# Handing more of the fp32 split to GpSimd, and spacing the router's steps, in a two-block transformer kernel

## The chip, the cores and the metric

The kernel runs on one core of one Trainium2 chip. The metric is the device time of one execution in microseconds (us), as a median over runs; smaller is better.

## The reference, cut to what matters

Two blocks work on 256 tokens of width 1024. The change touches only the PEER feed-forward that closes each of the two layers of the second block (128 x 128 experts, 8 heads, 16 experts per head):

```
def peer_ffn(x, w_query, sub_keys, down, up):      # T = 256, H = 8, K = 16
    q = (xt @ w_query).reshape(T, H, 2, 64)
    s = einsum('thcd,cnd->thcn', q, sub_keys)      # scores of 2 x 128 keys
    sv, si = top_k(s, K)
    cand_s = (sv[:, :, 0, :, None] + sv[:, :, 1, None, :]).reshape(T, H, K * K)
    cand_i = (si[:, :, 0, :, None] * 128 + si[:, :, 1, None, :]).reshape(T, H, K * K)
    top_s, pos = top_k(cand_s, K)
    idx, gate = take_along_axis(cand_i, pos), softmax(top_s)
    a = einsum('thkd,td->thk', down[idx], x)       # down, up: 16384 x 1024
    c = gate * gelu(a)
    return einsum('thk,thkd->td', c, up[idx])
```

## The kernel before, in words

**Weights as slots.** All weights are streamed from HBM in the order of their use and cut into 765 slots of 128 x 1024 fp32. Every slot is split into a high part `whi` (ScalarE copies the raw slot to fp32r, `hi`, L312) and a low part `wlo` (raw minus high, `lo`, L331). TensorE then multiplies three products per tile (`three`, L349 to L351). There are three buffers of `whi` and `wlo`, so the split of slot i waits until TensorE has used slot i-3. The low part is made by VectorE, except for the slots named in the set `ON_POOL`, which GpSimd (POOL) makes; both engines walk through the slots in order. GpSimd has nothing else to do in the PEER stages until they end.

**The PEER stage** of a layer has 264 slots, from 201 in layer 0 and from 501 in layer 1: 8 of `w_query`, then 128 of `down`, then 128 of `up`. The experts are not gathered: all 16384 activations are computed. In the down phase a loop over pairs p = 0 to 63 takes slots i = 209 + 2p and i + 1 (layer 0), and ScalarE puts the gelu of the result into `AST` (L2606). In the up phase the loop runs over 62 pairs and a tail; ScalarE (`CH`, L2589) and VectorE (`CL`, L2808) split the scaled activations for each pair. `ON_POOL` holds, in layer 0, slots 212 to 239 and every second slot from 339 to 401.

**Routing** runs beside the down phase. `route_at(p)` names the steps that VectorE takes in pair p, after its `lo(i+3)` and `lo(i+4)`:

- `keys(q, 1..5)`, q = 0 to 3: top 16 of the key scores, with MAX8, FIND_INDEX8, MATCH_REPLACE8. TensorE supplies the scores by `scores(q)` (L2484).
- `pick(tt, 0..5)` for each half tt of the tokens: `CD` (sums of candidates, L2690 to L2696), their top 16, and in segment 5 `TB` (L2704), the scores less the largest.
- ScalarE takes the exponential of that (`pick(tt, 5)`, L2576).
- `pick(tt, 6)` waits for it and then normalizes; segments 7 to 9 and 11 to 13 turn positions into expert numbers with `count` (L2670, L2674): 60 small instructions per tt, each with two inputs in SBUF.
- TensorE turns the three tables over (`tables(tt)`, L2494), after pairs 22 and 29. It works in order: what comes behind in its queue waits for VectorE's last `count` and the copy L2759. ScalarE copies the turned tables out after pairs 23 and 30, and VectorE splits the gates in segment 20 at pairs 24 and 31.

**Gates.** From pair 32 on, in down and up, `gates(s)` for 64 groups of 8 tokens: TensorE L2504, then on VectorE L2799 (`AST` times gates) and `build(s+2)` (`OI` L2782, `EQ` L2786, `OJ` L2791). `gates_at` names the pairs; in three of them (n = 47, 74, 84) there are two groups.

Of the kernel before, what the change touches and what calls it, by code (L numbers as in the profile page):

```python
# [67 lines left out]
ON_POOL = set(range(1, 14, 2)) | set(range(71, 100, 2))  # L68
for _s in (165, 465):
    ON_POOL |= set(range(_s + 2, _s + 31, 2))  # L70
for _s in (201, 501):
    ON_POOL |= set(range(_s + 11, _s + 39)) | set(range(_s + 138, _s + 202, 2))


class Book:
# [81 lines left out]
class Program:  # L157
# [2274 lines left out]
        t.spill = self.nc.dram_tensor(f"x_spill{l}", (P, 2 * D), F32, kind="Internal").ap()  # L2432
        return t

    def route_at(self, p):

        if p < 10:
            return [("keys", s // 5, s % 5 + 1) for s in (2 * p, 2 * p + 1)]  # L2440
        if p < 14:
            tt = (p - 10) // 2
            return [("pick", tt, 3 * (p % 2) + s) for s in range(3)]
        if p < 28:
            tt = (p - 14) // 7
            return [("pick", tt, (6, 7, 8, 9, 11, 12, 13)[(p - 14) % 7])]
        return []

    def gates_at(self, n):

# [23 lines left out]
    def peer_pe(self, e, t):  # L2474
        k, PS, n, tag = self.k, self.ps, t.n, t.tag
        self.norm_turned(n)

        def scores(q):
            tt, half = q // 2, q % 2
            for h in range(4 * half, 4 * half + 4):  # L2480
                b = 4 + h // 2
                for w in k.late((tag, "qh", h), (tag, "sk in"), *(self.free[b] if h % 2 == 0 else [])):
                    e.wait_ge(*w)
                m = e.matmul(PS[:, b, (h % 2) * 256:(h % 2) * 256 + 256], t.QH[:, h, tt * 128:tt * 128 + 128], t.SK[:, :],  # L2484
                             start=True, stop=True)
                self.free[b] = [(tag, "keys", q, 5, 7)]
            m.then_inc(*k.inc("pe_keys", (tag, "scores", q)))

        def tables(tt):
            self.bank(e, 2 + tt)  # L2490
            for j, what in enumerate(("oi", "oj", "g")):
                for w in k.late((tag, what, tt)):
                    e.wait_ge(*w)
                m = e.transpose(PS[:, 2 + tt, 128 * j:128 * j + 128], t.TB[:, tt, j, :], self.ident[:, :])  # L2494
            m.then_inc(*k.inc("pe_keys", (tag, "tables turned", tt)))
            self.free[2 + tt] = [(tag, "table", tt, 2)]

        def gates(s):
            b = 2 + s % 2
            for w in k.late((tag, "one i", s), (tag, "one j", s, 0), (tag, "one j", s, 1), *self.free[b]):  # L2500
                e.wait_ge(*w)
            for x in range(8):
                for p in range(2):
                    m = e.matmul(PS[:, b, 64 * x:64 * x + 64], t.OI[s % 2][:, x // 2, :, x % 2], t.OJ[s % 2][:, p, x // 2, :, x % 2],  # L2504
                                 start=p == 0, stop=p == 1)
            m.then_inc(*k.inc("pe_gates", (tag, "gates", s)))
            self.free[b] = [(tag, "scaled", s)]

        def query(h):
            b = h % 2 if h > 1 else 4 + h  # L2510
            if h == 0:
                self.chan_pair(e, t.slot, n, [PS[:, x, 0:T] for x in (4, 5)], [4, 5])
            elif h > 1:
                self.bank(e, b)
                self.chan(e, t.slot + h, n, PS[:, b, 0:T])
            self.free[b] = [(tag, "qh", h)]

        for h in range(8):
            query(h)
        scores(0)  # L2520
        for p in range(64):
            b, i = p % 2, t.down + 2 * p
            self.bank(e, b)
            self.chan(e, i, n, PS[:, b, 0:T])
            self.chan(e, i + 1, n, PS[:, b, T:2 * T], ahead=p == 63)
            self.free[b] = [(tag, "gelu", p)]
            if p in (1, 4, 6):
                scores((1, 4, 6).index(p) + 1)
            if p in (22, 29):
                tables(p // 29)  # L2530
            for s in self.gates_at(p):
                gates(s)
        rows = (tag, t.up, t.CH, t.CL, range(128), lambda c: [(tag, "ch", c // 2), (tag, "cl", c // 2)], (4, 5, 6, 7))
        for p in range(62):
            for s in self.gates_at(64 + p):
                gates(s)
            for x in range(2):
                self.rows_main(e, *rows, 2 * p + x)
        self.rows_main(e, *rows, 124)
        self.rows_first(e, *rows)  # L2540
        self.rows_second(e, *rows)
        for h in range(2):
            self.rows_third(e, *rows, h)
        self.free[4:8] = [[("x", n + 1, tt, h)] for tt in range(2) for h in range(2)]
        if t.l == 0:
            for tt in range(2):
                self.norm_turn(e, n + 1, tt)
# [7 lines left out]
    def peer_act(self, e, t):  # L2555
        k, PS, n, tag = self.k, self.ps, t.n, t.tag
# [12 lines left out]
                self.hi(e, t.slot + 4)  # L2569

        def pick(tt, seg):
            if seg == 5:
                g = t.TB[:, tt, 2, :].rearrange("p (h k) -> p h k", k=16)
                for w in k.late((tag, "less", tt)):
                    e.wait_ge(*w)
                e.activation(g, g, ACT.Exp, bias=0.0, scale=1.0).then_inc(*k.inc("act_keys", (tag, "exp", tt)))  # L2576
            if seg == 19:
                q = slice(128 * tt, 128 * tt + 128)
                for j, (o, scale) in enumerate(((t.IT, 1.0), (t.JT, 1.0), (t.GF, SCALE))):
                    for w in k.late((tag, "tables turned", tt), (tag, "spilled"), ("hl", n, 7)):  # L2580
                        e.wait_ge(*w)
                    e.activation(o[:, q], PS[:, 2 + tt, 128 * j:128 * j + 128], ACT.Copy, bias=0.0,
                                 scale=scale).then_inc(*k.inc("act_keys", (tag, "table", tt, j)))
# [10 lines left out]
        for p in range(64):  # L2594
            b, i = p % 2, t.down + 2 * p
            self.hi(e, i + 3)
            if p == 63:
                part(0)
                part(1)
            self.hi(e, i + 4)  # L2600
            late = [(tag, "keys", 3, 5, 7)] if 2 * p == t.on_keys else []
            if 2 * p == t.on_tables:
                late = [(tag, "tables", 0), (tag, "tables", 1)]
            for w in k.late(("used", i + 1), *late):
                e.wait_ge(*w)
            e.activation(t.AST[:, p, :, :].rearrange("p t a -> p a t"), PS[:, b, :].rearrange("p (a t) -> p a t", a=2),  # L2606
                         ACT.Gelu_apprx_tanh, bias=0.0, scale=1.0).then_inc(*k.inc("act_down", (tag, "gelu", p)))
            if p in (11, 13):
                pick(p // 13, 5)
            if p in (23, 30):  # L2610
                pick(p // 30, 19)
        for p in range(62):
            part(p + 2)
            for x in range(2):
# [7 lines left out]
    def peer_dve(self, e, t):  # L2622
        k, PS, n, tag = self.k, self.ps, t.n, t.tag
# [52 lines left out]
        def pick(tt, seg):  # L2676
            s = t.SV[:, tt, :, :].rearrange("p (h c) k -> p h c k", c=2)
# [20 lines left out]
            if 1 <= seg < 6:  # L2698
                best((tag, "top", tt), seg - 1, lambda r: cd[:, r, :], lambda r: t.TV[:, tt, r, :], lambda r: t.PI[:, tt, r, :],
                     lambda r: cd[:, r, :], range(8), [(tag, "sums", tt)])  # L2700
            if seg == 5:
                for w in k.late((tag, "top", tt, 4, 7)):
                    e.wait_ge(*w)
                e.tensor_tensor(g, t.TV[:, tt, :, :], t.TV[:, tt, :, 0:1].to_broadcast([P, 8, 16]),  # L2704
                                ALU.subtract).then_inc(*k.inc("dve_pick", (tag, "less", tt)))
            if seg == 6:
                for w in k.late((tag, "exp", tt)):
                    e.wait_ge(*w)
                e.tensor_reduce(t.sm[:, tt, 0:8], g, AX, ALU.add).then_inc(*k.inc("dve_pick", (tag, "total", tt)))
# [43 lines left out]
                k.same((*col, "sum", -2), (*col, "sum", -1))  # L2753
            if 11 <= seg < 14:
                count(tt, col, range(1, 16), 1, 5 * (seg - 11))
            if seg == 13:
                for w in k.late((*col, "sum", 14)):
                    e.wait_ge(*w)
                e.tensor_copy(oj, acc).then_inc(*k.inc("dve_pick", (tag, "oj", tt)))  # L2759
            if seg == 20:  # L2760
                q = slice(128 * tt, 128 * tt + 128)
# [51 lines left out]
        for p in range(64):  # L2813
            i = t.down + 2 * p
            self.lo(e, i + 3)
            if p == 63:
                part(0)
                part(1)
            self.lo(e, i + 4)
            for kind, q, seg in self.route_at(p):  # L2820
                (keys if kind == "keys" else pick)(q, seg)
            if p in (24, 31):
                pick(p // 31, 20)
            if p == 31:
                build(0)
                build(1)
            for s in self.gates_at(p):
                gates(s)
# [288 lines left out]
```

## Time and profile before

| what | before |
|---|---|
| median of 3 runs | 2531.83 us (2531.47 to 2534.66) |
| profiled execution: its time / span | 2534.66 us / 2532.8 us |
| TensorE busy | 2441.3 us (96%) |
| VectorE busy | 1816.0 us (72%) |
| ScalarE busy | 1192.0 us (47%) |
| GpSimd busy | 536.9 us (21%) |
| the PEER stages | about 765 to 1560 us and 1740 to 2533 us |

TensorE's time is close to the whole; the other engines' shares are averages over stages in which they have quite different loads.

### The profile page before, as it was taken

To read this page: it belongs to the slowest core of one execution; us is meant where nothing else is said; L and a number is where in the kernel's file an instruction comes from. 1 tells how busy PE (TensorE), PEld (TensorE's weight loads), DVE (VectorE), ACT (ScalarE), POOL (GpSimd) and SP (SyncE) were. 2 spreads that over 40 slices of the span, in tenths; PEclk is the share of its full clock that TensorE was granted. 3 is DMA by queue.
4 is the path that set the end of the run, shared out by engine and by line. 5 is a ranking of instruction groups with operands and counts; after the bars stand their busy time and mean duration, and the time that the engine had idled before them with its cause. 6 is when DMAs were issued, how large, how long until landed. Compare 5 with 4: busy or idle time off the path is not lost.

```text
span 2532.8 us, 43179 instructions
## 1 busy us (share of the span) xinstructions
PE 2441.3 (96%) x17718; PEld 2224.5 (88%) x17718; DVE 1816.0 (72%) x3408; ACT 1192.0 (47%) x1665; POOL 536.9 (21%) x374
## 2 busy tenths in 40 slices
PE   7999798998999999999999999999999999999999
PEld 7987778987879999999778887888999999877887
DVE  8787946656545687777998555745777777999555
ACT  3545545445445544444444555454454444444444
POOL 3023321003423700001333001340720000333000
PEclk9999999999999999999999999999999999999999
DMA  9696534654324455444445555324455444444554
GB/s 386 205 374 220 183 114 160 216 201 156 117 100 169 170 180 184 167 167 167 167 164 195 196 197 181 113 101 152 168 184 182 169 166 167 172 169 174 202 197 150
DMA packets 73045, 456.03 MB, mean 180 GB/s; under 512 B 9099, under 2 KB 15371, under 8 KB 20754
## 3 DMA queue, kind: packets, MB, share of 16 engines
q1 hardware_dynamic: 72162, 452.21, 49.8%
q8 instruction: 142, 2.33, 0.4%
q0 software_dynamic: 688, 1.06, 0.3%
q14 instruction: 53, 0.43, 0.0%
HBM read 449.17 MB, written 4.06 MB: 179 GB/s over the span
## 4 chain that ended last, share of the span: by engine, by line
PE 75%; DVE 18%; ACT 3%; issue 2%; POOL 1%; DMA 0%; SPq 0%; DVEq 0%; POOLq 0%; ACTq 0%
PE ps L349 23%; PE ps L351 23%; PE ps L350 23%; DVE OI L2782 4%; DVE wlo L331 3%; PE ps L2504 2%; DVE AST L2799 1%; DVE raw L342 1%; DVE CL L2808 1%; ACT whi L312 1%; PE ps L377 1%; DVE OJ L2791 1%; DVE XB L1182 1%; DVE EQ L2786 1%; ACT xn L454 1%
## 5 line engine op out<-in xcount | busy, mean ns | idle before, releaser
L312 ACT ACTIVATE whi<-raw 128x1024 fp32r<-128x1024 f32 x765 | 809.6, 1060 | 1143.8 <-PE ps L351 1094.4
L331 DVE TENSOR_TENSOR wlo<-raw,whi 128x1024 fp32r<-128x1024 f32 x593 | 736.6, 1245 | 522.7 <-ACT whi L312 522.3
L349 PE MATMUL ps<-HH,whi 128*128 128x256 f32 x3016 | 867.5, 288 | 8.2 <-DVE wlo L331 4.4
L350 PE MATMUL ps<-HL,whi 128*128 128x256 f32 x3016 | 856.6, 284 | 0.0
L351 PE MATMUL ps<-HH,wlo 128*128 128x256 f32 x3016 | 856.4, 284 | 0.0
L331 POOL TENSOR_TENSOR wlo<-raw,whi 128x1024 fp32r<-128x1024 f32 x172 | 421.5, 2451 | 1167.4 <-ACT whi L312 1167.4
L349 PEld LDWEIGHTS ps<-HH,whi 128*128 128x128 f32 x3016 | 580.4, 192 | 13.8 <-issue 8.4
L350 PEld LDWEIGHTS ps<-HL,whi 128*128 128x128 f32 x3016 | 580.7, 193 | 0.8
L351 PEld LDWEIGHTS ps<-HH,wlo 128*128 128x128 f32 x3016 | 580.3, 192 | 0.5
L349 PE MATMUL ps<-whi,CH 128*128 128x512 f32 x1024 | 405.3, 396 | 7.3 <-DVE wlo L331 7.3
L350 PE MATMUL ps<-wlo,CH 128*128 128x512 f32 x1024 | 400.0, 391 | 0.0
L351 PE MATMUL ps<-whi,CL 128*128 128x512 f32 x1024 | 400.0, 391 | 0.0
L349 PEld LDWEIGHTS ps<-whi,CH 128*128 128x128 f32 x1024 | 193.1, 189 | 47.0 <-ACT whi L312 8.9
L351 PEld LDWEIGHTS ps<-whi,CL 128*128 128x128 f32 x1024 | 193.0, 188 | 40.6
L350 PEld LDWEIGHTS ps<-wlo,CH 128*128 128x128 f32 x1024 | 193.2, 189 | 38.2
L2782 DVE TENSOR_TENSOR OI<-iota,IT 128x1024 f16<-128x1024 bf16 x128 | 182.7, 1427 | 0.0
L2808 DVE SCALAR_TENSOR_TENSOR CL<-AST,CH 128x512 fp32r<-128x512 f32 x128 | 101.5, 794 | 9.2 <-ACT CH L2589 8.9
L462 POOL TENSOR_SCALAR st<-st 128x1 f32<-128x1 f32 x20 | 9.8, 492 | 460.8 <-ACT xn L454 258.8
L2791 DVE TENSOR_TENSOR OJ<-EQ,GP 128x512 f16<-128x512 f16 x256 | 97.4, 421 | 4.4
L342 DVE CUSTOM_DVE_ANT_0 raw<-raw,cb 128x1024 f32<-128x1024 f32 x72 | 92.2, 1318 | 0.0
L2799 DVE TENSOR_TENSOR AST<-AST,ps 128x512 f32<-128x512 f32 x128 | 87.0, 680 | 6.2 <-PE ps L2504 4.2
L349 PE MATMUL ps<-whi,HH 128*128 128x256 f32 x288 | 85.1, 296 | 0.0
(390 smaller groups left out, 2735.5 us busy)
## 6 DMA issues: line engine op xcount, KB each, us to landing
raw<-in_down SPq DMA_DIRECT2D x128, 1024.0 KB, 4.8
raw<-in_up SPq DMA_DIRECT2D x128, 1024.0 KB, 4.8
raw<-in_w_in SPq DMA_DIRECT2D x41, 1024.0 KB, 4.8
raw<-in_ffn_gu SPq DMA_DIRECT2D x36, 1024.0 KB, 5.0
raw<-in_w_ada SPq DMA_DIRECT2D x28, 1024.0 KB, 6.7
raw<-in_ffn_d SPq DMA_DIRECT2D x22, 1024.0 KB, 5.6
raw<-in_w_out SPq DMA_DIRECT2D x12, 1024.0 KB, 4.8
raw<-in_w_ada SPq DMA_DIRECT2D x16, 512.0 KB, 13.3
```

What stands on the lines that cost most here:

```text
L312: e.activation(self.whi[:, i % NSPLIT, :], self.raw_of(i), ACT.Copy, bias=0.0, scale=1.0).then_inc(*k.inc("w_hi", ("hi", i)))
L331: e.tensor_tensor(self.wlo[:, n, :], self.raw_of(i), self.whi[:, n, :].bitcast(F32), ALU.subtract).then_inc(*k.inc("w_lo_pool" if pool els ...
L342: e.tensor_tensor_reduce(out=raw[:, a, :], in0=raw[:, a, :], in1=self.cb[:, :], scale=1.0, scalar=0.0, op0=ALU.mult, op1=ALU.add, accum_ou ...
L349: e.matmul(out, lh, rh, start=first, stop=False)
L350: e.matmul(out, lh, rl, start=False, stop=False)
L351: return e.matmul(out, ll, rh, start=False, stop=stop)
L377: t = e.matmul(outs[j], part[:, s], h[:, c, :], start=first and not (j and one), stop=stop and (j == 1 or not one))
L2504: m = e.matmul(PS[:, b, 64 * x:64 * x + 64], t.OI[s % 2][:, x // 2, :, x % 2], t.OJ[s % 2][:, p, x // 2, :, x % 2], start=p == 0, stop=p == 1)
L2782: e.tensor_tensor(t.OI[c][:, :, :, :], self.iota[:, :, :].unsqueeze(1).to_broadcast([P, 4, 128, 2]), spread(t.IT, 128), ALU.is_equal).then ...
L2791: e.tensor_tensor(t.OJ[c][:, p, :, :, :], t.EQ[:, :, :, :], spread(t.GP[:, p, :], 64), ALU.mult).then_inc(*k.inc("dve_gates", (tag, "one j ...
L2799: e.tensor_tensor(c, c, PS[:, b, :].rearrange("p (t j a) -> p j t a", a=2, j=32), ALU.mult).then_inc(*k.inc("dve_gates", (tag, "scaled", s)))
L2808: e.scalar_tensor_tensor(lo, t.AST[:, p, :, :].rearrange("p t a -> p a t"), 1.0 / SCALE, hi.bitcast(F32), ALU.mult, ALU.subtract).then_inc ...
```

## The change

`ON_POOL` grows in the PEER stages: in layer 0 from 212..239 and every second slot of 339..401 to all slots 213..275 and every second one of 277..453 (first slot of each pair). Slot 212 goes to VectorE. Layer 1 is the same, 300 slots later.

The routing steps get another order in time: `route_at(n)` gives the steps 2n+1 and 2n+2 of one list, of 24 steps of `keys` (6 for each q) and 42 of `pick` (21 for each tt). So `scores(1..3)` come after pairs 2, 5, 8 (before: 1, 4, 6), the exponentials after pairs 14 and 25 (before: 11, 13), `tables(0)` and `tables(1)` after pairs 20 and 30 (before: 22, 29), ScalarE's copies after 21 and 31 and segment 20 at pairs 21 and 32 (before: 24, 31). Segment 6 now holds both `TB` and the normalization, L2759 stands in segment 14. The instructions themselves stay the same. On VectorE, all of `pick(1, ..)` now comes behind segment 20 of tt 0; before, segments 0 to 5 of tt 1 came ahead of segment 6 of tt 0, and `TB` ahead of each wait for the exponential by a pair or more.

```
 for _s in (201, 501):
-    ON_POOL |= set(range(_s + 11, _s + 39)) | set(range(_s + 138, _s + 202, 2))
+    ON_POOL |= set(range(_s + 12, _s + 75)) | set(range(_s + 76, _s + 253, 2))
...
-    def route_at(self, p):
-        if p < 10:
-            return [("keys", s // 5, s % 5 + 1) for s in (2 * p, 2 * p + 1)]
-        if p < 14:
-            tt = (p - 10) // 2
-            return [("pick", tt, 3 * (p % 2) + s) for s in range(3)]
-        if p < 28:
-            tt = (p - 14) // 7
-            return [("pick", tt, (6, 7, 8, 9, 11, 12, 13)[(p - 14) % 7])]
-        return []
+    def route_at(self, n):
+        out = []
+        for s in (1 + 2 * n, 2 + 2 * n):
+            if s < 24:
+                out.append(("keys", s // 6, s % 6))
+            elif s < 66:
+                out.append(("pick", (s - 24) // 21, (s - 24) % 21))
+        return out
...
-            if p in (1, 4, 6):
-                scores((1, 4, 6).index(p) + 1)
-            if p in (22, 29):
-                tables(p // 29)
+            for kind, q, seg in self.route_at(p):
+                if kind == "keys" and seg == 0:
+                    scores(q)
+                if kind == "pick" and seg == 17:
+                    tables(q)
...
-            if p in (11, 13):
-                pick(p // 13, 5)
-            if p in (23, 30):
-                pick(p // 30, 19)
+            for kind, q, seg in self.route_at(p):
+                if kind == "pick":
+                    pick(q, seg)
...
-            if seg == 5:
+            if seg == 6:
...
-            if seg == 6:
...
-            if seg == 13:
+            if seg == 14:
...
-            if p in (24, 31):
-                pick(p // 31, 20)
```

## Rows read from the trace of the kernel before

**Rows 1.** Windows: engines' busy time, TensorE's granted clock, DMA share, GB/s.
```profile
818.00:860.00 42.00, 42.00 (x339) 41.59 (x339) 31.10 (x204) 18.24 (x21) 31.94 (x15) 1.00 0.49 171
1085.00:1184.00 99.00, 99.00 (x997) 98.36 (x996) 75.63 (x117) 41.13 (x47) 0.00 (x0) 1.00 0.47 169
1184.00:1250.00 66.00, 66.00 (x459) 54.04 (x458) 64.63 (x76) 30.57 (x36) 26.40 (x11) 1.00 0.48 171
1250.00:1320.00 70.00, 68.17 (x455) 54.79 (x453) 68.36 (x85) 29.13 (x33) 26.63 (x11) 0.98 0.44 156
```

**Rows 2.** Waits of the whole run: total us, times, longest us.
```profile
PE ps L349 <- DVE wlo L331: 11.7, 9, 2.6
```

**Rows 3.** Timeline of ScalarE (start, duration) in the down phase: gelu and exponential.
```profile
870.14 0.31 ACT L2576 ACTIVATE TB<-TB 128x128 f32<-128x128 f32 x1
...
914.29 0.62 ACT L2606 ACTIVATE AST<-ps 128x512 f32<-128x512 f32 x1
920.05 0.62 ACT L2606 ACTIVATE AST<-ps 128x512 f32<-128x512 f32 x1
```

**Rows 4.** Costliest groups of the page: count, busy us, mean ns.
```profile
L312 ACT ACTIVATE whi<-raw 128x1024 fp32r<-128x1024 f32 x765 | 809.6, 1060 | 1143.8 <-PE ps L351 1094.4
```

**Rows 5.** Timeline of GpSimd in the down phase, with idle time before each.
```profile
848.16 2.52 POOL L331 TENSOR_TENSOR wlo<-raw,whi 128x1024 fp32r<-128x1024 f32 x1 [0.41 <-ACT whi L312]
851.11 2.40 POOL L331 TENSOR_TENSOR wlo<-raw,whi 128x1024 fp32r<-128x1024 f32 x1 [0.42 <-ACT whi L312]
...
856.86 2.40 POOL L331 TENSOR_TENSOR wlo<-raw,whi 128x1024 fp32r<-128x1024 f32 x1 [0.55 <-ACT whi L312]
```

**Rows 6.** Timeline of VectorE over the same stretch.
```profile
847.87 2.96 DVE L2690 TENSOR_TENSOR CD<-SV 128x128 f32<-128x128 f32 x5
...
851.11 1.00 DVE L2632 MAX8 TV<-CD 128x8 f32<-128x50 f32 x8
...
857.36 2.06 DVE L2704 TENSOR_TENSOR TB<-TV 128x128 f32<-128x128 f32 x1
```

**Rows 7.** Timeline of VectorE: one pair of count, the last copy.
```profile
892.78 0.29 DVE L2670 SCALAR_TENSOR_TENSOR T<-PF,DL 128x128 f32<-128x128 f32 x1
893.11 0.29 DVE L2674 TENSOR_TENSOR AC<-AC,T 128x128 f32<-128x128 f32 x1
893.32 0.28 DVE L2670 SCALAR_TENSOR_TENSOR T<-PF,DL 128x128 f32<-128x128 f32 x1
...
924.08 0.23 DVE L2759 COPY TB<-AC 128x128 f32<-128x128 f32 x1
```

**Rows 8.** Groups of VectorE's instructions, 870 to 980 us: busy us, mean ns.
```profile
L331 DVE TENSOR_TENSOR wlo<-raw,whi 128x1024 fp32r<-128x1024 f32 x34 | 41.2, 1222 | 28.1 <-ACT whi L312 28.0
L2674 DVE TENSOR_TENSOR AC<-AC,T 128x128 f32<-128x128 f32 x60 | 17.5, 292 | 2.1
L2670 DVE SCALAR_TENSOR_TENSOR T<-PF,DL 128x128 f32<-128x128 f32 x60 | 17.1, 284 | 0.1
```

**Rows 9.** Timeline of TensorE: the tables of the first tt.
```profile
930.35 0.49 PE L2494 MATMUL ps<-ident,TB 128*128 128x128 f32 x3
```

**Rows 10.** Windows after idle time of TensorE, at its lower clock.
```profile
301.00:313.00 12.00, 3.14 (x24) 2.94 (x24) 11.80 (x15) 2.58 (x4) 5.51 (x2) 0.82 0.64 231
313.00:319.00 6.00, 5.47 (x22) 4.49 (x23) 4.78 (x13) 4.92 (x10) 0.00 (x0) 0.50 0.15 63
1257.00:1261.00 4.00, 3.52 (x9) 2.79 (x10) 3.96 (x8) 0.00 (x0) 0.00 (x0) 0.58 0.63 221
```

**Rows 11.** Groups: building the one-hot tables without GpSimd (down) and beside it (up).
```profile
L2782 DVE TENSOR_TENSOR OI<-iota,IT 128x1024 f16<-128x1024 bf16 x17 | 11.6, 685 | 0.0
L2782 DVE TENSOR_TENSOR OI<-iota,IT 128x1024 f16<-128x1024 bf16 x11 | 28.4, 2580 | 0.0
```

**Rows 12.** Timeline of VectorE where two groups of gates fall in one pair.
```profile
1253.92 3.41 DVE L331 TENSOR_TENSOR wlo<-raw,whi 128x1024 fp32r<-128x1024 f32 x1
```

**Rows 13.** Timeline of GpSimd at the same place.
```profile
1253.54 2.71 POOL L331 TENSOR_TENSOR wlo<-raw,whi 128x1024 fp32r<-128x1024 f32 x1 [4.14 <-ACT whi L312]
```

More of the change, by code:

```diff
@@ L2700, in pick @@
                      lambda r: cd[:, r, :], range(8), [(tag, "sums", tt)])
-            if seg == 5:
+            if seg == 6:
                 for w in k.late((tag, "top", tt, 4, 7)):
```

## The prediction, made before the change was run

> **What bounds the kernel now.** I read the windows over the stretches of one PEER stage first [rows 1]. TensorE is busy for all of the 42, 99 and 66 us of the first three, so in the down phase (with routing, then with gates) and at the start of the up phase it is the bound. Next the waits [rows 2]: TensorE's waits for a low part come to 11.7 us in the whole run. So the work that the change lifts from VectorE is work for which hardly anything waits. The gain to be had is small, and what counts is whether somebody new becomes late. A pair takes 5.76 us in the down phase (920.05 less 914.29) [rows 3], a slot 2.88 us.
>
> **What GpSimd's split does to VectorE.** GpSimd takes 2.40 us for one slot [rows 5], where VectorE takes 1.22 us [rows 8]. If it makes every slot, it is busy for 2.40 of 2.88 us and leaves gaps of 0.41 to 0.55 us [rows 5]. TensorE stayed busy in that regime [rows 1], so GpSimd's own pace is no loss. Now lay the two timelines side by side [rows 5, 6]. `TB`, 128 elements, starts on VectorE at 857.36 and takes 2.06 us, to 859.42; GpSimd's split ran from 856.86 to 859.26. A `count` instruction of 128 elements takes 0.28 to 0.29 us [rows 8]. So `TB` stood still until GpSimd had ended and finished 0.16 us later. The five `CD` sums took 2.96 us, to 850.83, 0.15 us behind the end of the split at 850.68. The one-hot `OI` shows the same: 0.685 us without GpSimd, 2.58 us beside it [rows 11]. These instructions read two operands from SBUF. MAX8, with one input, ran its eight in 1.00 us right beside a split [rows 6].
>
> The Trainium skill ("SBUF — State Buffer", Who interferes with whom) states this as a rule: a VectorE instruction with two SBUF inputs and a GpSimd instruction that reads SBUF exclude each other, the first keeps the shared ports for its whole length, and the other one blocks. The trace agrees (2.06 against 0.29 us).
>
> **Part 1, slots 213 to 275 on GpSimd.** Slots 240 to 275 are the new ones; they are needed during pairs 15 to 33. Just there VectorE runs the `count` chains, 60 instructions with two SBUF inputs for each tt. Before, no split of GpSimd's ran beside them. Saved on VectorE: 36 x 1.22 = 44 us per layer, worth nothing on TensorE's path, since it did not wait there. What it costs, for each tt:
>
> - The work between the exponential and the tables: 30 pairs of `count` at 0.54 us (892.78 to 893.32) [rows 7] are 16.2 us, and 15 other small instructions at about 0.26 us are 3.9 us: 20.1 us in 75 instructions, some 0.27 us each, if nobody is in the way.
> - How much of it goes through while GpSimd works: in each cycle of 2.88 us the gap is 0.48 us. The blocked instruction goes first, a second follows, at times a third; then GpSimd has the ports again. It isn't kept out by a queue of small instructions: in the middle of the five `CD` GpSimd's split came out at 2.52 us, 0.12 us over the usual 2.40 [rows 5]. So 2 to 3 instructions per cycle. From the `CD` sums alone one could read 4, but all but the first of these have 24 to 64 elements (8 heads by 3 to 8); I take 2.25 of 128 elements, 0.6 us of work, and keep 2 (0.53 us) and 4 (1.06 us) as bounds.
> - tt 0: the exponential is made after pair 14 instead of 11, so it ends at 870.45 + 3 x 5.76 = 887.7 us [rows 3]. TensorE comes to `tables(0)` two pairs earlier than at 930.35 [rows 9], at 918.8 us. When it stops there, one more slot is copied (1.06 us [rows 4]) and split (2.40 us) before GpSimd falls idle for want of a free buffer: 3.5 us. By then 31.1 + 3.5 = 34.6 us have passed, 12 cycles, with 12 x 0.6 = 7.2 us of work. 12.9 us are left, and VectorE does them at its full speed, since GpSimd stands still. **Wait of TensorE: 3.5 + 12.9 = 16.4 us.**
> - tt 1: now all of `pick(1, ..)` waits behind segment 20 of tt 0, but the exponential after pair 25 still comes later than its input: from the resumption at about 935 us, pair 21 and ScalarE's table take to about 945, segment 20, the sums and four rounds of MAX8 and its kin some 15 us more, and pair 25 ends near 966. The exponential ends 3.4 us behind its pair (870.45 against 930.35 - 11 x 5.76 = 867.0) [rows 3, 9], `tables(1)` stand five pairs on: 28.8 - 3.4 = 25.4 us, and 3.5, are 10 cycles with 6.0 us of work. 14.1 us are left. **Wait: 17.6 us.**
> - After each wait TensorE starts at half its clock. After 12 us in which it was busy for 3.14 only, the window from 313 to 319 us shows 0.50, the 1.2 GHz level, for nearly 6 us; from 1257 to 1261 us, after one of the short stalls of part 3, it is 0.58, or 3.4 of 4 us at the lower level [rows 10]. I estimate 3.4 to 5.4 us at half speed after each wait, a loss of half of that, 1.7 to 2.7 us; I take 2.4.
>
> Per layer 16.4 + 17.6 + 4.8 = 38.8 us. Layer 1 has the same instructions at the same relative times. Two layers: **77.6 us**.
>
> **Part 2, the spacing of the steps.** `scores(1..3)` one to two pairs later and the exponential three pairs later cost nothing by themselves: VectorE was through with tt 0 at 924.3 us [rows 7], 6 us ahead of the tables. But these 6 us, the cover, are used up: without any blocking, tt 0 would be ready at 887.7 + 20.1 = 907.8, 11 us ahead of the tables at 918.8. With blocking it would need over 90 us. The spacing, which shortens the time to the tables, thus adds to part 1; it costs nothing without it. Slot 212 on VectorE delays `keys(0)` by a few us; the banks of `scores(2)` are asked for only after pair 5. Nothing.
>
> **Part 3, every second slot from 277 to 335, beside the gates.** VectorE has one split less (1.22 us) and up to one blocked `OI` more (2.58 against 0.69, 1.9 us) per pair; a pair with gates lasts 6.3 us. Behind the waiting `OI` stand `EQ`, `OJ` and the next low part. In the up phase just this arrangement, with `CL` on top, left TensorE busy for 66 of 66 us [rows 1], with less time per pair. So nothing; if the pair with two groups (n = 47) stalls as the ones in the up phase do, where a low part on VectorE took 3.41 us behind GpSimd's split [rows 12, 13], that is 1.83 us idle (70 less 68.17 [rows 1]) and 1.7 us for the clock, 3.5 us per layer, 7 in all.
>
> **Part 4, every second slot from 403 to 453.** VectorE is lightly loaded there; a blocked `CL` costs it under 2 us in a pair and saves one split. Nothing.
>
> **Sum.** The profiled execution took 2534.7 us, its span 2532.8; it is the slowest of the three runs, 2.8 us above the median. Its span plus 77.6 is 2610, against the median 2531.8 + 77.6 = 2609 us. With 4 instructions per cycle the waits are 10.8 and 12.9 us, and with 1.7 for the clock the sum is 2 x 27.1 = 54, so 2586. With 2 per cycle 17.2 and 18.3, with 2.7 for the clock and 7 us of part 3 it is 2 x 40.9 + 7 = 89, so 2621.
>
> **The rivals.**
>
> - *The small instructions aren't held.* Only larger or strided ones would wait. Then tt 0 is ready at 907.8 us, ahead of the tables, and nothing changes: 2532 us. For it: the first of the five `CD` passed. Against it: `TB`, 128 elements just like `count`. One page of the Trainium skill ("Advanced Engine Details and Errata", Mode Summary) has a note that names only VectorE's two-port modes as interfering with GpSimd, which would leave the fp32 additions of `count` alone; this trace speaks against reading it so.
> - *GpSimd is the one kept out.* If the chain of `count` holds the ports from end to end, GpSimd loses 20.1 us per tt, TensorE has two slots in hand (5.8 us) and waits 14.3 us for low parts: 4 x (14.3 + 2.4) = 67, 2599 us. Against it: the split of 2.52 us. It differs in what TensorE is seen waiting for.
> - *Faster.* The four stalls of a doubled group of gates, 1.8 us and about 1.7 us for the clock each, 14 us in all, might go, if another phase between VectorE and GpSimd let the low part through: 2518 us. It decides only if the tables don't wait at all. The slots there are assigned as before, so nothing asks for it.
>
> **How the numbers follow.** The forecast, waits at the tables that add 54 to 89 us: 0.78. GpSimd kept out, 2599: 0.08. Not held, 2532: 0.09. Faster, 2518: 0.03. Another cause of a smaller loss: 0.02. What a measurement of this kernel can tell from no change is about 0.2%, 5 us. Faster 0.03, same 0.09, slower 0.88. The range is the forecast's with some room above for what follows late tables (the first `build`s): 2580 to 2632. It leaves out the unchanged and the faster case, and a little on either side.
>
> **What would show it.** TensorE idle for 12 to 18 us ahead of L2494, twice in each layer; `count` instructions of about 2.5 us between 888 and 920 us, some two per split of GpSimd's, then a run of undisturbed ones while TensorE and GpSimd stand still. The down phase with gates without idle time of TensorE. The prediction is wrong if TensorE is found waiting for low parts, if `count` keeps its 0.28 us beside GpSimd, or if 5 or more get through in each gap.

## The result, and the profile after

| | before | after |
|---|---|---|
| median | 2533.24 us (4 runs) | 2606.99 us (4 runs) |
| profiled execution: time / span | 2534.66 / 2532.8 us | 2605.91 / 2603.7 us |
| ratio, 95% interval | | 1.0292 (1.028 to 1.0305) |

Slower by 74 us, against a forecast of 77 (2609 us). In the profiled executions the span grew by 70.9 us. One execution of e9 below ran in a slower state (2672.52 us at a granted clock of 0.843, the others at 0.984 to 0.987); it counts in the median of e9 but not in its ratio. Line numbers differ by a few between the kernels: `tables` is L2494 before and L2491 here, `count` L2670 and L2674 before, L2667 and L2671 here.

The page of the changed kernel, engine by engine:

```profile
PE 2451.5 (94%) x17718; PEld 2232.7 (86%) x17718; DVE 1926.8 (74%) x3224; ACT 1191.3 (46%) x1665; POOL 1012.4 (39%) x558
```

GpSimd has 476 us more, and VectorE, from which 184 splits were taken, is busy for 111 us more instead of less. The timelines below show why: an instruction that stands still counts as busy. TensorE's waits for the tables, which were not in the list of before (total us, times, longest):

```profile
PEld ps L2491 <- DVE TB L2755: 36.2, 4, 9.1
PE ps L2491 <- DVE TB L2755: 35.0, 4, 8.8
PEld ps L2491 <- DVE TB L2738: 25.8, 4, 7.2
PE ps L2491 <- DVE TB L2738: 25.0, 4, 7.0
```

The timeline of TensorE, layer 0, answers to [rows 9]; the number in brackets is the idle time ahead. `tables` first waits for the row numbers (`TB` of L2738), then for the column numbers (L2755):

```profile
924.30 0.48 PE L2491 MATMUL ps<-ident,TB 128*128 128x128 f32 x1 [5.51 <-DVE TB L2738]
933.53 0.69 PE L2491 MATMUL ps<-ident,TB 128*128 128x128 f32 x2 [8.75 <-DVE TB L2755]
999.82 0.47 PE L2491 MATMUL ps<-ident,TB 128*128 128x128 f32 x1 [7.00 <-DVE TB L2738]
1009.05 0.69 PE L2491 MATMUL ps<-ident,TB 128*128 128x128 f32 x2 [8.76 <-DVE TB L2755]
```

So 14.3 us for tt 0 and 15.8 us for tt 1, 30.0 us in this layer. The waits of the whole run are 60.0 us, so layer 1 has 30.0 us too. Of the 70.9 us of the span 10.9 are left, 5.4 per layer. Nearly all of that is the clock: for the same 17718 matmuls TensorE is busy for 10.2 us more than before (2451.5 against 2441.3), 5.1 per layer, where the forecast had 4.8. The windows around and behind the two waits, and the stretch of gates in the down phase (busy time of PE, PEld, DVE, ACT and POOL, then the granted clock, as in [rows 1]):

```profile
918.00:935.00 17.00, 2.73 (x15) 2.24 (x14) 14.58 (x44) 1.57 (x2) 4.02 (x2) 0.64 0.18 62
934.00:940.00 6.00, 6.00 (x44) 6.00 (x43) 0.00 (x0) 1.06 (x1) 0.73 (x1) 0.80 0.01 3
1012.00:1018.00 6.00, 6.00 (x41) 6.00 (x41) 0.46 (x2) 1.16 (x2) 1.96 (x1) 0.76 0.01 3
1085.00:1185.00 100.00, 100.00 (x1028) 99.31 (x1027) 91.64 (x101) 41.40 (x48) 44.35 (x16) 1.00 0.47 164
```

And what VectorE and GpSimd do ahead of the wait (VectorE's timeline, then its groups and GpSimd's between 887.5 and 918.5 us), to lay beside [rows 7, 8]:

```profile
908.47 0.28 DVE L2667 SCALAR_TENSOR_TENSOR T<-PF,DL 128x128 f32<-128x128 f32 x1
908.79 2.38 DVE L2671 TENSOR_TENSOR AC<-AC,T 128x128 f32<-128x128 f32 x1
911.09 0.28 DVE L2667 SCALAR_TENSOR_TENSOR T<-PF,DL 128x128 f32<-128x128 f32 x1
911.40 2.46 DVE L2671 TENSOR_TENSOR AC<-AC,T 128x128 f32<-128x128 f32 x1
913.79 0.28 DVE L2667 SCALAR_TENSOR_TENSOR T<-PF,DL 128x128 f32<-128x128 f32 x1
```

```profile
L2671 DVE TENSOR_TENSOR AC<-AC,T 128x128 f32<-128x128 f32 x12 | 14.0, 1168 | 0.4
L2667 DVE SCALAR_TENSOR_TENSOR T<-PF,DL 128x128 f32<-128x128 f32 x12 | 12.2, 1020 | 0.0
```

```profile
L331 POOL TENSOR_TENSOR wlo<-raw,whi 128x1024 fp32r<-128x1024 f32 x12 | 29.3, 2443 | 5.3 <-ACT whi L312 5.3
```

Two or three instructions go through for each split, and one of them carries the length of the split. In 31 us VectorE gets 24 of its 60 `count` instructions done, where an undisturbed chain needs 16 us for all 60. GpSimd's last split before the stop runs from 920.01 to 922.45 us. Behind it the chain runs free, while TensorE and GpSimd stand still, to the copy that TensorE waits for:

```profile
922.64 0.29 DVE L2671 TENSOR_TENSOR AC<-AC,T 128x128 f32<-128x128 f32 x1
...
932.92 0.29 DVE L2671 TENSOR_TENSOR AC<-AC,T 128x128 f32<-128x128 f32 x1
933.25 0.23 DVE L2755 COPY TB<-AC 128x128 f32<-128x128 f32 x1
```

### The profile page after: what moved, and what is told of

It is laid out like the page before. It is cut to its first block, busy times and chain, and to the rows that moved or that the text cites. A ratio compares the mean times of both kernels' runs of the same rounds, so it can differ in the third digit from the quotient of the medians.

```text
span 2603.7 us, 43291 instructions
## 1 busy us (share of the span) xinstructions
PE 2451.5 (94%) x17718; PEld 2232.7 (86%) x17718; DVE 1926.8 (74%) x3224; ACT 1191.3 (46%) x1665; POOL 1012.4 (39%) x558
## 4 chain that ended last, share of the span: by engine, by line
PE 68%; DVE 24%; ACT 3%; issue 2%; POOL 1%; DMA 1%; SPq 0%; DVEq 0%; POOLq 0%; ACTq 0%
PE ps L349 21%; PE ps L351 20%; PE ps L350 20%; DVE OI L2778 4%; DVE wlo L331 3%; DVE AC L2671 3%; DVE T L2667 3%; PE ps L2501 2%; ACT whi L312 1%; DVE AST L2795 1%; DVE raw L342 1%; DVE CL L2804 1%; DVE OJ L2787 1%; PE ps L377 1%; DVE EQ L2782 1%
## 5 line engine op out<-in xcount | busy, mean ns | idle before, releaser
L331 POOL TENSOR_TENSOR wlo<-raw,whi 128x1024 fp32r<-128x1024 f32 x356 | 894.3, 2512 | 1047.8 <-ACT whi L312 1047.7
L331 DVE TENSOR_TENSOR wlo<-raw,whi 128x1024 fp32r<-128x1024 f32 x409 | 511.9, 1253 | 270.3 <-ACT whi L312 269.8
L2804 DVE SCALAR_TENSOR_TENSOR CL<-AST,CH 128x512 fp32r<-128x512 f32 x128 | 191.5, 1497 | 102.9 <-ACT CH L2587 102.6
L2782 DVE TENSOR_TENSOR EQ<-iota,JT 128x512 f16<-128x512 bf16 x128 | 197.0, 1539 | 0.0
```

The source lines that it names most:

```text
L331: e.tensor_tensor(self.wlo[:, n, :], self.raw_of(i), self.whi[:, n, :].bitcast(F32), ALU.subtract).then_inc(*k.inc("w_lo_pool" if pool els ...
L2782: e.tensor_tensor(t.EQ[:, :, :, :], self.iota[:, js, :].unsqueeze(1).to_broadcast([P, 4, 64, 2]), spread(t.JT, 64), ALU.is_equal).then_inc ...
L2804: e.scalar_tensor_tensor(lo, t.AST[:, p, :, :].rearrange("p t a -> p a t"), 1.0 / SCALE, hi.bitcast(F32), ALU.mult, ALU.subtract).then_inc ...
```

## The experiments

Ten kernels, beside the kernel before on the same chip. `before` stands for that kernel, `after` for the changed one; medians in us, ratios to before.

| kernel | median | ratio (95%) |
|---|---|---|
| e1: GpSimd's slots alone | 2577.35 | 1.018 (1.0163 to 1.0197) |
| e2: spacing alone | 2558.45 | 1.0101 (1.0083 to 1.0118) |
| e3: after, 240..275 back on VectorE | 2559.63 | 1.0106 (1.0089 to 1.0123) |
| e4: after, every second of 240..275 | 2575.16 | 1.0165 (1.0148 to 1.0182) |
| e5: after, operands in PSUM | 2549.77 | 1.0063 (1.0048 to 1.0078) |
| e8: e1, operands in PSUM | 2536.76 | 1.0007 (0.9998 to 1.0016) |
| e6: before, two slots more per layer | 2538.67 | 1.0017 (1.0008 to 1.0026) |
| e7: before, slots swapped | 2522.30 | 0.9956 (0.9942 to 0.9969) |
| e9: e8 with the swap of e7 | 2524.49 | 0.9954 (0.994 to 0.9969) |
| e10: before, slots beside gates and at the end | 2534.88 | 1.0002 (0.9994 to 1.0011) |

### e1: GpSimd's new slots alone

```diff
-    ON_POOL |= set(range(_s + 11, _s + 39)) | set(range(_s + 138, _s + 202, 2))
+    ON_POOL |= set(range(_s + 12, _s + 75)) | set(range(_s + 76, _s + 253, 2))
```

> The new set of GpSimd's slots alone, with the steps of the router spaced as before. If small instructions with two SBUF inputs stand still during a split (the theory), the tables are still late: VectorE starts tt 0 at 886.8 us, TensorE asks for them at 930.4, and 47 us at 0.6 us of work per 2.88 us leave 10 us to do, a wait of 14 us; much the same for tt 1; with the clock 33 us per layer, about 2598 us. If it was the spacing of the steps that cost the time (first rival), this kernel takes about 2532 us.

Measured 2577 us: not 2532, so the slots alone make the tables late, but 21 us less than worked out. The timeline shows the two waits of layer 0:

```profile
937.90 0.69 PE L2494 MATMUL ps<-ident,TB 128*128 128x128 f32 x2 [7.65 <-DVE TB L2759]
988.75 0.69 PE L2494 MATMUL ps<-ident,TB 128*128 128x128 f32 x2 [8.25 <-DVE TB L2759]
```

The expectation let VectorE begin the tables' work at 886.8 us, as before. It begins at 870.5, right behind ScalarE's exponential:

```profile
870.50 0.27 DVE L2709 TENSOR_REDUCE sm<-TB 128x8 f32<-128x128 f32 x1
...
871.25 2.43 DVE L2717 CAST PF<-PI 128x128 f32<-128x128 uint32 x1
...
873.91 2.54 DVE L2721 TENSOR_TENSOR DL<-SF 128x240 f32<-128x240 f32 x1
...
876.94 2.37 DVE L2670 SCALAR_TENSOR_TENSOR T<-PF,DL 128x128 f32<-128x128 f32 x1
```

With no low part of its own between the steps, nothing ties VectorE to the pair that TensorE is in, and the written order gives no times any more.

### e2: the new spacing of the router's steps alone

```diff
-    ON_POOL |= set(range(_s + 12, _s + 75)) | set(range(_s + 76, _s + 253, 2))
+    ON_POOL |= set(range(_s + 11, _s + 39)) | set(range(_s + 138, _s + 202, 2))
```

(in after)

> The new spacing of the steps alone, with GpSimd's slots as before. The theory: 2532 us, within 5, since VectorE has its 20 us of work for tt 0 done by about 913 us, before TensorE asks at 918.8. The first rival (the spacing costs the time: tables asked for sooner, tt 1 wholly behind tt 0): about 2607 us, with idle time of TensorE ahead of the tables.

Neither: 2558 us. TensorE does not wait for tables but, between 880 and 1000 us, for low parts:

```profile
PE ps L349 <- DVE wlo L331: 7.0, 5, 2.4
PEld ps L349 <- ACT whi L312: 4.9, 3, 1.7
PEld ps L349 <- issue: 4.4, 3, 2.6
PE ps L349 <- ACT whi L312: 1.2, 1, 1.2
```

VectorE's timeline there shows why:

```profile
900.84 2.35 DVE L331 TENSOR_TENSOR wlo<-raw,whi 128x1024 fp32r<-128x1024 f32 x2
903.11 0.28 DVE L2667 SCALAR_TENSOR_TENSOR T<-PF,DL 128x128 f32<-128x128 f32 x1
...
905.53 0.29 DVE L2671 TENSOR_TENSOR AC<-AC,T 128x128 f32<-128x128 f32 x1
905.74 2.35 DVE L331 TENSOR_TENSOR wlo<-raw,whi 128x1024 fp32r<-128x1024 f32 x2
```

The new spacing puts two segments of `count` (5.3 us) beside two splits (2.3 us) into a pair of 5.76 us; the old one put one segment there. The waits of the matmuls themselves sum to 8.2 us in this stage (7.0 and 1.2; those of `PEld` are the same gaps seen from the weight load); the span grew by 22.7 us, 11.3 per layer, and not all of it comes from the spacing. Counted from the first gelu of a layer (`AST`, L2606 before, L2604 here), the growth is 2.2 us ahead of the gelu of layer 0 (803.27 against 801.10 us), where the kernels do not differ, 7.9 from there to that of layer 1 (980.80 against 972.94), and 12.7 from there to the end (771.43 against 758.76). Layer 0 is thus accounted for by its waits; layer 1 has the same 8.2 us, and TensorE is busy for 4.4 us more, with a granted clock of 0.72 between 1896 and 1902 and between 2252 and 2258 us, where layer 1 of the kernel before shows no such drop.

### e3: the changed kernel without slots 240 to 275

```diff
-    ON_POOL |= set(range(_s + 12, _s + 75)) | set(range(_s + 76, _s + 253, 2))
+    ON_POOL |= set(range(_s + 12, _s + 39)) | set(range(_s + 76, _s + 253, 2))
```

> The changed kernel, but slots 240 to 275 of a layer back on VectorE; the slots beside the gates and at the end of the up phase stay on GpSimd. The theory: the whole loss goes, 2532 us within 5. Second rival (the blocked one-hot builds or CL beside the new slots from 277 on cost part of it): above 2540 us; every stall of a low part in the down phase would show as idle time of TensorE between 990 and 1184 us.

2560 us, 20 us above the bound named for the second rival, but for another reason: the waits are those of e2 (7.0 us for low parts between 880 and 1000 us), and between 990 and 1184 us TensorE has no idle time. Against e2 it is 1.2 us. As a test of the slots beside the gates it was badly built, since the new spacing costs 25 us by itself once VectorE makes the low parts; e10 repeats it cleanly.

### e4: every second one of slots 240 to 275

```diff
-    ON_POOL |= set(range(_s + 12, _s + 75)) | set(range(_s + 76, _s + 253, 2))
+    ON_POOL |= set(range(_s + 12, _s + 39)) | set(range(_s + 40, _s + 253, 2))
```

> The changed kernel, with only every second one of slots 240 to 275 on GpSimd. The theory: per pair of 5.76 us GpSimd holds the ports for 2.4 us and VectorE's own split takes 1.2, so 2.1 us are left for the router's work of 20.1 us; at the tables 9 to 11 us of it are left, waits of about 10 us each, and with the clock about 2580 us (2568 to 2590). If only an almost full GpSimd does harm (third rival: the gaps close when it is busy for 2.4 of 2.88 us), about 2532 us.

2575 us, within the range, but the path is not the expected one. There is no wait at the tables; between 880 and 1000 us TensorE waits for VectorE's low parts:

```profile
PEld ps L349 <- issue: 15.6, 5, 3.4
PE ps L349 <- DVE wlo L331: 14.8, 5, 3.2
```

The held `count` chains now stand in front of low parts in VectorE's own queue:

```profile
894.13 2.50 DVE L2667 SCALAR_TENSOR_TENSOR T<-PF,DL 128x128 f32<-128x128 f32 x1
...
899.84 2.46 DVE L2671 TENSOR_TENSOR AC<-AC,T 128x128 f32<-128x128 f32 x1
...
903.26 1.22 DVE L331 TENSOR_TENSOR wlo<-raw,whi 128x1024 fp32r<-128x1024 f32 x1
```

The time is no support for my working. It does answer the third rival: GpSimd is busy for only 2.4 of 5.76 us here, its split still holds a `count` instruction for 2.5 us, and the kernel is 17 us slower than e2, which has the same spacing.

### e5 and e8: one input of each count instruction in PSUM

```diff
-        t.DL = a("DL", [P, 2, 8, 2, 16])
+        t.DL = [self.ps[:, 4 + tt, 0:256].rearrange("p (h c k) -> p h c k", c=2, k=16) for tt in range(2)]
+        t.T1 = [[self.ps[:, 6 + tt, 128 * j:128 * j + 128] for j in range(2)] for tt in range(2)]
-        t.AC, t.T1 = a("AC", [P, 2, 128]), a("T1", [P, 2, 2, 128])
+        t.AC = a("AC", [P, 2, 128])
```

(The lines of the buffers alone. `DL` is an input of the first instruction of each `count` pair; `T1` is its output and an input of the second.)

> The changed kernel with DL and T1, one operand of each of the 120 count instructions of a layer, held in PSUM: the same instructions, GpSimd's slots and spacing. The theory (two operands in SBUF make an instruction stand still during a split): count takes about 0.3 us each again; of the 75 instructions of a tt some 15 still have two operands in SBUF or are held copies, 5 to 6 cycles of 2.9 us, so the tables are ready at 915 to 925 us and TensorE waits 0 to 7 us each: 2532 to 2560, about 2545 us. Rival (a split slows any VectorE instruction of a chain, wherever its operands lie): 2605 us again.

> The same move to PSUM in the kernel with the new set of GpSimd's slots and the old spacing (2577 us so far, tables late by 7.7 and 8.3 us). The theory: VectorE is ready with the tables of tt 0 by about 905 us, 25 us early: 2532 us within 5. Rival as before: 2577 us.

e5: 2550 us, 57 us better than after, 5 above the point expected and within the range. VectorE's groups between 887.5 and 918.5 us, and GpSimd's:

```profile
L2668 DVE SCALAR_TENSOR_TENSOR ps<-PF,ps 128x128 f32<-128x128 f32 x30 | 8.7, 291 | 0.1
L2672 DVE TENSOR_TENSOR AC<-AC,ps 128x128 f32<-128x128 f32 x30 | 8.6, 288 | 1.0
L2742 DVE SCALAR_TENSOR_TENSOR TB<-TB,AC 128x128 f32<-128x128 f32 x1 | 2.5, 2450 | 0.0
L2748 DVE TENSOR_SCALAR AC<-SF 128x128 f32<-128x128 f32 x1 | 2.4, 2386 | 0.0
```

```profile
L331 POOL TENSOR_TENSOR wlo<-raw,whi 128x1024 fp32r<-128x1024 f32 x12 | 28.9, 2405 | 5.7 <-ACT whi L312 5.7
```

Beside the same 12 splits all 60 `count` instructions run, at 0.29 us, and GpSimd's splits are back at 2.405 us from 2.443. What stands still in this stretch has its inputs in SBUF: two of them (L2742) or, in two `TENSOR_SCALAR`s, only one (L2748). The 16 us that e5 is still above the kernel before have a place: the tables of tt 0 are ready in time (916.8 us), those of tt 1 are late by 3.6 us in each layer, and the clock follows.

```profile
PE ps L2492 <- DVE TB L2756: 7.2, 2, 3.6
```

e8 has the move with the old spacing: TensorE never waits for tables, and of e1's 44 us 3.3 are left; the interval holds 1. In the profiled execution of e8 even these arise before the PEER stages: its first gelu comes at 804.56 instead of 801.10 us, and from there to the end both kernels take 1731.6 to 1731.7 us. This settles the mechanism: same instructions, same order, same splits, another place of one input. (In the first instruction of a pair the output moved as well; in the second, L2672, only the input did, and it is at 0.288 us just the same.)

### e10: the slots beside the gates and at the end, alone

```diff
-    ON_POOL |= set(range(_s + 11, _s + 39)) | set(range(_s + 138, _s + 202, 2))
+    ON_POOL |= set(range(_s + 11, _s + 39)) | set(range(_s + 76, _s + 253, 2))
```

> The kernel before with only the slots beside the gates (every second one of 277 to 335) and at the end of the up phase (403 to 453) added to GpSimd's. The forecast priced these two parts at nothing: 2533 us within 5. Second rival (the blocked one-hot builds make a low part or a group of gates late): more than 2540 us.

No difference (1.0002), as priced. One of the builds is held in each pair, `EQ` and not `OI` as forecast (groups of VectorE, 1085 to 1184 us), and TensorE is busy for all 99 us:

```profile
L2786 DVE TENSOR_TENSOR EQ<-iota,JT 128x512 f16<-128x512 bf16 x17 | 40.3, 2370 | 0.0
L2782 DVE TENSOR_TENSOR OI<-iota,IT 128x1024 f16<-128x1024 bf16 x17 | 13.2, 779 | 0.0
```

### e6, e7 and e9: the stalls that were there before

```
e6 (in before): ON_POOL |= {_s + 159, _s + 179}
e7 (in before): ON_POOL ^= {_s + 159, _s + 160, _s + 179, _s + 180}
e9 (in e8):     the line of e7
```

> The kernel before, with two slots of a layer more on GpSimd, 360 and 380, the next low parts in the two pairs of the up phase with a doubled group of gates. The theory: their low part is late since VectorE comes to it 0.4 us behind the start of GpSimd's next split (1253.9 against 1253.5 us) and is held for 2.2 us; on GpSimd it is made before that. Two stalls of 1.8 us and their clock go in each layer, up to 14 us: 2520 us. Rival: two splits in a row on GpSimd hold the one-hot builds, and the stall moves to another wait: 2532 us or more.

> The same, but GpSimd and VectorE swap slots in these pairs: 360 and 380 to GpSimd, 361 and 381 to VectorE, so that GpSimd makes no split more than before. The theory: 2520 us as well, rather surer than with two splits in a row. Rival: the wait moves to another place, 2532 us.

> The new set of GpSimd's slots with the old spacing, DL and T1 in PSUM, and the swap of the two slots per layer that brought the kernel before to 2522 us. TensorE is then bound by its own work throughout, so the 72 slots more on GpSimd can't add anything: 2522 to 2526 us, the same as the swap alone within 5 us. If the relief of VectorE were worth something once nothing is late, it would be under 2518 us.

e7, the swap, gives 2522 us, 11 us under the kernel before, and the window of [rows 1] that had 68.17 us of work in 70 is full:

```profile
1250.00:1320.00 70.00, 70.00 (x484) 56.90 (x483) 69.51 (x92) 30.90 (x35) 29.14 (x11) 1.00 0.48 173
```

The 11 us can be added up from the kernel before. Its four stalls are 1.83 us each, 7.3 in all. Behind the two of layer 0 the granted clock falls (0.58 from 1257 to 1261 us, [rows 10]; 0.91 over the 20 us around each, 1.8 us lost each time). Behind the two of layer 1 it does not:

```profile
2230.00:2234.00 4.00, 3.57 (x29) 2.94 (x30) 3.96 (x8) 0.23 (x1) 0.00 (x0) 1.00 0.64 221
```

That makes 10.9 us. e6, which gives GpSimd one slot more there and takes none away, gains nothing and is 5 us slower (1.0017): the rival. In its timeline splits hold `EQ` and `OJ`, and VectorE comes to its next low part only at 1265.01 us, for which TensorE now waits 2.55 us:

```profile
1255.95 2.62 DVE L2786 TENSOR_TENSOR EQ<-iota,JT 128x512 f16<-128x512 bf16 x1
...
1261.53 2.95 DVE L2791 TENSOR_TENSOR OJ<-EQ,GP 128x512 f16<-128x512 f16 x2
...
1265.01 1.21 DVE L331 TENSOR_TENSOR wlo<-raw,whi 128x1024 fp32r<-128x1024 f32 x1
```

e9 is level with e7 (ratios 0.9954 and 0.9956). TensorE's waits for VectorE between the gelus and the end of a PEER stage are down to 0.3 us in each layer, and the low parts that GpSimd makes on top of those of before bring nothing. They are 92 per layer (558 instructions of GpSimd against 374, two layers), not the 72 of the expectation.

## Why the prediction was right, point by point

- *TensorE is the bound, so relief of VectorE is worth nothing.* Right: e10 (1.0002) and e9 against e7.
- *Part 1, the held chains.* The mechanism was right, and e5 and e8 show it. The times of the path came out within 0.2 us: VectorE starts at 887.57 us (887.7 forecast) and TensorE stops at 918.79 (918.8). The size was somewhat off: waits of 14.3 and 15.8 us instead of 16.4 and 17.6. The term was the work that passes per cycle. Of the instructions from the exponential to the tables 32 had started by 918.5 us, beside 12 splits, 2.7 for each; I took 2.25. With 2.7, 0.27 x 2.7 = 0.73 us of work in each of 12 and 10 cycles leaves 11.3 and 12.8 us, waits of 14.8 and 16.3 us. This working uses the result and is no second test.
- *The clock.* 5.4 us per layer are left over, and TensorE's busy time grew by 5.1; 4.8 forecast. The sum was about right, an equal 2.4 for each wait was not: TensorE runs at half speed for 2.9 us behind the first wait of layer 0 (933.5 to 936.4, a loss of 1.4) and for 5.8 us behind the second (1009.1 to 1014.9, a loss of 2.9).
- *The total.* For the spans the forecast was 77.6 and the result 70.9 us. That the medians differ by 74, nearer to the forecast, is a matter of the executions: the profiled one of the kernel before was above its median.
- *Part 2, the spacing.* "It costs nothing without it" was wrong. e2 shows 25 us. The check that I had not made is whether a pair's work on VectorE still fits the pair: two segments and two low parts are 7.6 us in 5.76. In the changed kernel this cost is absent, since VectorE makes hardly any low part there; instead the spacing moves the exponential by three pairs and the tables by two. After less e1 is 30 us. Nearly all of them are waits at the tables (60.0 us in the whole run against 31.5 in e1). That e1 (44 us) and e2 (25 us) add up to 69, near to 74, is chance, for after has no wait for a low part between 796 us and the up phase.
- *Part 3 and part 4.* Nothing, as forecast; the held build is another one.
- *The rivals.* Small instructions are held (e5). GpSimd is not kept out: its splits went from 2.40 to 2.44 us. The faster case did not come by itself, but its price was real: e7 gets 11 of the 14 us that were put on those four stalls. The rest is the clock term, put on all four and seen behind two.

Left open: why `EQ` and not `OI` is held in the down phase (it would follow from when the split starts, but no run moved that), and why the same 1.83 us of idle time is followed by the lower clock in layer 0 and not in layer 1.

## What to carry to other kernels

Work taken from an engine that nobody waits for gains nothing, and what the receiving engine does to its neighbours can cost much. Before giving GpSimd a stream of two-input work, list VectorE's instructions with two operands in SBUF in that stretch, above all dependent chains of small ones with a deadline: with GpSimd busy for 2.4 of every 2.9 us, only 2 to 3 of them passed per cycle, a slowdown of about four (2.88 us for 2.7 instructions of 0.27 us). And before spacing steps more tightly, add up what VectorE has to do in each pair: in e2 VectorE is busy for 71% of the span, yet single pairs ask 7.6 us of work of it in 5.76. Two remedies were measured here: one operand in PSUM, or the choice of which engine takes the slot that is urgent.

## What the runs showed of the hardware that was not expected

- A `TENSOR_SCALAR` from SBUF to SBUF with one input (L2748 in e5) was held as well, for 2.39 us instead of 0.23, and a cast for 2.43 us in e1; MAX8 (before, [rows 6]) and the `count` instructions with one input in PSUM were not. So the number of SBUF inputs alone does not say who is held. The Trainium skill ("SBUF — State Buffer", Who interferes with whom) names copies, casts and scalar instructions in a two-port mode as the other class that excludes GpSimd. These durations agree with that; no run changed the operands of these instructions to test it.
- Turn and turn about is not an even share of the delay: in the changed kernel GpSimd's splits lengthened by 0.04 us on average, while `count` went from 0.28 and 0.29 us to 1.02 and 1.17 us.
